# Last output projections by token half: all features of half 0, then all of half 1

## The reference, cut to what matters

```python
for layer in range(DEPTH):
    h = rmsnorm(x, norm_g[layer])
    y = mixer(h, ...)          # each ends in (o * silu(g)) @ w_out
    x = x + y
return rmsnorm(x, final_g)
```

## Time and profile before

| | |
|---|---|
| median of 3 runs | 3079.87 us (3074.44 to 3081.11) |
| the profiled execution | 3079.59 us, span 3077.9 us |
| instructions | 43530 |
| DVE, ACT, POOL busy | 56%, 40%, 20% |
| mean granted clock of PE | 0.927 |
| DMA | 107.89 MB, mean 35 GB/s |
| `w_out` slabs loaded | 8 + 16 + 8 + 8, of 512 KB each |

### The profile page before, as it was taken

One profiled execution on the slowest core, in us unless ns is written; L12 is line 12 of the kernel. 1 busy time (PEld: TensorE's weight loads), 2 busy tenths in 40 slices (PEclk: granted clock), 3 DMA queues, 4 the chain that ended last, 5 costly groups with the idle time before them and its releaser, 6 DMA issues. The chain is left out here.

```text
span 3077.9 us, 43530 instructions
## 1 busy us (share of the span) xinstructions
PE 2506.3 (81%) x17488; PEld 1421.7 (46%) x17488; DVE 1715.5 (56%) x2387; ACT 1242.4 (40%) x1857; POOL 607.9 (20%) x457
## 2 busy tenths in 40 slices
PE   4899878667887977978896888888888779888887
PEld 1566643224544544545553344444344235655543
DVE  5455453465555555555544676676676434455543
ACT  3322332233443433433432566666666423333221
POOL 2000001210000000000022455555555420000001
PEclk8999999788999999999997899999999889999988
DMA  2111000100010000010102110111111001111001
GB/s 83 35 41 36 29 28 28 50 26 13 24 32 30 27 31 19 31 38 15 43 14 62 28 49 28 49 49 42 28 49 35 14 29 35 35 35 35 28 28 69
DMA packets 43036, 107.89 MB, mean 35 GB/s; under 512 B 7986, under 2 KB 13362, under 8 KB 42836
## 3 DMA queue, kind: packets, MB, share of 16 engines
q1 hardware_dynamic: 42836, 105.11, 11.0%
HBM read 84.11 MB, written 4.19 MB: 29 GB/s over the span
## 5 line engine op out<-in xcount | busy, mean ns | idle before, releaser
L219 PE MATMUL psum<-h_hi,gla_w_hi 128*128 128x512 f16 (+1 forms) x544 | 215.9, 397 | 93.0 <-issue 47.8
L1417 ACT ACTIVATE mla_prob<-psum,mla_neg_top 128x128 f32<-128x128 f32 (+7 forms) x128 | 94.9, 741 | 343.3 <-DVE mla_neg_top L1322 343.3
L918 POOL TENSOR_TENSOR sb_al<-sb_zc,sb_ah 128x256 f16<-128x256 f32 (+2 forms) x96 | 171.8, 1790 | 220.5 <-ACT sb_ah L873 220.5
L220 PE MATMUL psum<-h_lo,gla_w_hi 128*128 128x512 f16 (+1 forms) x544 | 215.0, 395 | 0.0
L221 PE MATMUL psum<-h_hi,gla_w_lo 128*128 128x512 f16 (+1 forms) x544 | 214.4, 394 | 0.0
L1339 DVE TENSOR_TENSOR mla_pt_lo<-psum,mla_pt_hi 128x128 f16<-128x128 f32 (+7 forms) x128 | 97.0, 758 | 193.4 <-ACT mla_pt_hi L1425 193.4
L907 POOL TENSOR_TENSOR sb_zc<-sb_zc,sb_el 128x256 f32<-128x256 f32 (+2 forms) x96 | 174.6, 1818 | 137.5 <-ACT sb_el L850 137.4
L1480 POOL TENSOR_TENSOR mla_y_lo<-mla_yt,mla_y_hi 128x512 f16<-128x512 f32 x32 | 37.0, 1157 | 770.8 <-ACT mla_y_hi L1433 770.8
L235 PE MATMUL psum<-gla_w_hi,h_hi 128*128 128x128 f16 x1024 | 173.8, 219 | 11.0 <-issue 11.0
L1211 PE MATMUL psum<-mla_ident,mla_prob 128*128 128x128 f32 x576 | 97.7, 303 | 100.5 <-DVE mla_prob L1334 99.6
L219 PE MATMUL psum<-h_hi,sb_w_hi 128*128 128x512 f16 x384 | 155.0, 404 | 24.9 <-DVE h_lo L384 24.9
(11 more groups left out here) (320 smaller groups left out, 7323.1 us busy)
## 6 DMA issues: line engine op xcount, KB each, us to landing
sb_wf<-in_sb_in SPq DMA_DIRECT2D x32, 512.0 KB, 3.6
gla_wf<-in_gla_v SPq DMA_DIRECT2D x16, 512.0 KB, 3.5
gla_wf<-in_gla_g SPq DMA_DIRECT2D x16, 512.0 KB, 3.5
gla_wf<-in_gla_out SPq DMA_DIRECT2D x16, 512.0 KB, 3.5
mla_wf<-in_mla_gate SPq DMA_DIRECT2D x16, 512.0 KB, 3.4
mla_wf<-in_mla_out SPq DMA_DIRECT2D x16, 512.0 KB, 3.6
xT<-in_x_T SPq DMA_DIRECT2D x8, 512.0 KB, 6.4
gla_wf<-in_gla_q SPq DMA_DIRECT2D x8, 512.0 KB, 3.4
```

The costliest lines, as they stand in the source:

```text
L219: pe.matmul(out, wh[:, w], act_hi[:, k, tok], start=(i == 0), stop=False)
L220: pe.matmul(out, wh[:, w], act_lo[:, k, tok], start=False, stop=False)
L918: pool.tensor_tensor(self.al[s % 2][:, :, off:HALF], self.zc[s % 3][:, :, off:HALF], self.ah[s % 2][:, :, off:HALF], ALU.subtract).then_in ...
L1417: act.activation(self.prob[t % 2][:, 0:w], self.pair(t)[:, 0:w], ACT.Exp, bias=self.neg_top[:, k], scale=self.SCALE, accum_out=self.total[ ...
```

## The change

The last output projection of every layer runs over all feature blocks for token half 0 first, and then over all for half 1. A slab then has one unit (layer 1: two), and every slab is loaded and split twice, once for each half. The first units that are opened early are now half 0 of blocks 0 and 1 (layer 1: 0, 1 and 2), and these belong to two slabs. `finish_items` gets a second bound: ("w", s) stands at the earliest right behind the last item of slab s-2. The buffers of the squares go by k and not by c, and the counts that ACT and POOL wait for follow the new order.

```diff
         for i, it in enumerate(items):
             if it[0] in ("u", "part"):
                 first.setdefault(self.units[it[1]][2], i)
+                last[self.units[it[1]][2]] = i
         for s in where:
-            moved.setdefault(first[s - 1] if s else 0, []).append(("w", s))
+            at = first[s - 1] if s else 0
+            if s >= self.NSPLIT:
+                at = max(at, last[s - self.NSPLIT] + 1)
+            moved.setdefault(at, []).append(("w", s))
...
         act.wait_ge(L.acc_free[b], L.turn[n])
-        i = 2 * k + c
         if k == 0:
             out = L.net.ssum[:, c * HALF:(c + 1) * HALF]
         else:
-            out = self.sq[c][:]
-            if k > 1:
-                act.wait_ge(self.sum_ready, i - 3)
+            out = self.sq[k % 2][:]
+            if k > 2:
+                act.wait_ge(self.sum_ready, self.sums_before(k - 1, c))
+            elif c:
+                act.wait_ge(self.sum_ready, self.sums_before(1, c))
...
+    def sums_before(self, k, c):
+        return c * (KD - 1) + k - 1
...
-        i = 2 * k + c
-        pool.wait_ge(self.sq_ready, i + 1)
-        if i >= 4:
-            pool.wait_ge(self.sum_ready, i - 3)
-        pool.tensor_tensor(s, s, self.sq[c][:], ALU.add).then_inc(self.sum_ready, 1)
+        pool.wait_ge(self.sq_ready, c * KD + k + 1)
+        if k > 1:
+            pool.wait_ge(self.sum_ready, self.sums_before(k, c))
+        pool.tensor_tensor(s, s, self.sq[k % 2][:], ALU.add).then_inc(self.sum_ready, 1)
...
         last = []
-        for k in range(KD):
-            last += L.slab(w_out[k], 1024, [("x", (k, c, True)) for c in range(2)], [5, 6, 7])
+        for c in range(2):
+            for k in range(KD):
+                last += L.slab(w_out[k], 1024, [("x", (k, c, True))], [5, 6, 7])
         early, last = L.open_early(L.cut(last, ("x",)), 2)
...
-    def out_items(self, group, part):
+    def out_items(self, group, part, halves=range(2)):
         final = group == MLA_HEADS // self.GROUP - 1
         items = self.L.slab(self.w["out"][group * 4 + part], 1024,
-                            [("x", (2 * part + k, c, final, group)) for k in range(2) for c in range(2)], self.ACC)
+                            [("x", (2 * part + k, c, final, group)) for k in range(2) for c in halves], self.ACC)
...
         tail = []
-        for part in range(4):
-            tail += self.out_items(MLA_HEADS // self.GROUP - 1, part)
+        for c in range(2):
+            for part in range(4):
+                tail += self.out_items(MLA_HEADS // self.GROUP - 1, part, (c,))
         early, tail = L.open_early(L.cut(tail, ("x",)), 3)
...
     def act_x(self, act, n):
         k, c, final, group = self.L.units[n][1]
-        if final and (k, c) in ((0, 0), (1, 0)):
+        if final and (k, c) in ((1, 0), (2, 0)):
             act.wait_ge(self.rlo, len(self.ropes))
```

More of the change, by code:

```diff
@@ L146, in finish_items @@
         first = {}
+        last = {}
         for i, it in enumerate(items):
@@ L1624, in build_items @@
         last = []
-        for k in range(KD):
-            last += L.slab(self.w["out"][k], 1024, [("x", (k, c, True)) for c in range(2)], self.ACC)
+        for c in range(2):
+            for k in range(KD):
+                last += L.slab(self.w["out"][k], 1024, [("x", (k, c, True))], self.ACC)
         early, last = L.open_early(L.cut(last, ("x",)), 2)
```

## The result

The changed kernel takes 3086.91 us (median of 7 runs, 3083.02 to 3089.5) against 3079.53 us (median of 7, 3074.44 to 3081.11) before. The ratio is 1.0026, its 95% interval 1.0015 to 1.0038: slower by 7.4 us in the medians, with 4.6 to 11.7 us inside the interval. The profiled execution took 3089.5 us, span 3087.8; it is the slowest of the seven, so the two profiles lie 9.9 us apart.

The account below looks back on a forecast made before the run. PE (TensorE) alone was taken to set the four output projections. Stalls of 5.4 us at the first units plus 1.6 for the clock gave +7.0, 3086.6 us; the 8-in-10 range was 3081.0 to 3093.0.

Parts of the forecast that it names:

- The waits: Before the third slab's first unit in each last output projection, PE idles until that slab is split: 5.4 us in sum.
- the wake-up: PE's restart after each of the four pauses: each could be 0.1 us more.
- The order among the waits: First gated 1.31, latent 0.6, stick-breaking 2.28, last gated 1.25 us; stick-breaking longest because the second unit's quarter ran at full clock.
- The steady part at nothing: Later units of the last projections: 28 more loads, high splits and low splits lie beside PE work and cost nothing.
- the cover of 1.19 us: Slack in each later unit: low split ends 3.99 us after the previous unit's end, next boundary comes at 5.18 us.
- the overrun rival: Later boundaries: split lag grows past 5.18 us and PE waits each time; 0.2 us at 48 boundaries, 3095; chance 0.05.
- The clock, one drop of three: After the three pauses over 1 us, one drops PE to half rate: +1.6 us.
- the lower bound of that term: Clock rises while PE idles, so matmuls run at full level later: -0.4 us per pause over 1 us, -1.2 together.
- The first rival: Only the stalls in the last projections, clock untouched: +5.4 us, 3085.0, counting as no change; chance 0.33.
- Early opening of C in the latent layer: The third unit's first quarter, opened early, finds the second slab already split, covered by 1.4 us: no cost.
- The rival on the other side: At layer boundaries the next norm takes half 0 early: 4.9 us at four boundaries, 3065.6; chance 0.04.
- The total: Whole kernel: stalls 5.4 plus clock 1.6 make +7.0 us, 3086.6 us.

Follow-up runs that it names:

- third pair: Changed kernel plus a third pair of split buffers for the last projections' slabs, all extra loads and splits kept: 3078.98 us against 3077.25 for the kernel before.
- loaded twice: Kernel before with its old order of units, but each slab of the last projections loaded and split once per unit: 3087.46 us, ratio 1.0034.

## Why the prediction was right, point by point

- **The waits.** Forecast 1.31, 0.6, 2.28 and 1.25 us, 5.4 in sum. Counted as the forecast counts, from A's add to C's first matmul (E's in the latent layer), the start moved by 1.36, 0.87, 2.39 and 1.30, 5.9 in sum. Three of the four are over by 0.05 to 0.11, the wake-up for which I had allowed 0.1 each. In the latent layer it is 0.27: I took 0.6 although the slower low split gave 0.75, and the slower one it was, 1.45 us. That PE's idle time in the four stretches is 5.4 too is chance: its brackets, 1.59, 0.70, 1.98 and 1.09, start later, and hang on when PE's clock rose during B's quarter. That the wait goes when the buffer does (third pair) and comes with the old order too (loaded twice) shows that it is this dependence.
- **The order among the waits** came out as well, the stick-breaking layer's longest, as B's quarter ran at the higher clock there.
- **The steady part at nothing.** In the gated and stick-breaking layers the cover of 1.19 us held: 1.1 us more in the chain cost nothing, 2.2 cost 0.47 at each boundary. For the latent layer the result is right and the reading wrong. I took 3.99 us of lag from the gated layer and wrote that 1.45 already holds the overlap with GpSimd; there it was 2.3, and 0.08 us of cover were left. That nothing was paid in this layer is luck, and the overrun rival, to which I gave 0.05, was near. Its form, an excess at each boundary, is the right one.
- **The clock, one drop of three.** The drop is in the stick-breaking layer, in all three profiles with this pause of 1.98 or 1.99 us (projection of 78.09 us each), and it costs 1.69 us; the pauses of the gated layers cost none. I had argued for a drop in this layer first, but one in three was a choice in the middle of a range, and that exactly one came is in part luck. In the last gated layer the shift gave back 0.4 (+1.30 at C, +0.88 at the end), the lower bound of that term: two matmuls that ran at 1.2 GHz now come after the rise. So the clock's net share is 1.3 us where I had 1.6, and the waits' 5.9 where I had 5.4: two small misses that partly cancel. The first rival, whose sum the Trainium skill's rule gave ("TensorE: Matmul & The Clock Gate", section "Why this matters for your kernels"), falls here: the page asks for a longer gap than the 1.98 us after which this clock was low, and filling that gap brought the clock back. The measurement decides. It is the trace that decides here: 5.4 us, the rival's sum, lie inside the interval of the times.
- **Early opening of C in the latent layer** waited for nothing: slab 1's low split ended at 1582.70, C's first matmul came at 1584.14, 1.4 us later, as forecast.
- **The rival on the other side,** that half 0 done early would let something start: as the code stood it could not, and the four stretches between a layer's last add and the next norm kept their length (4.85, 5.33, 7.09 and, before the final norm, 3.82 us before; 4.83, 5.32, 7.17 and 3.77 after). Not at the norm but in the branch output lay the gain of that order, and it took an edit of the wait and of the list to reach it: 16 us.
- **The total,** 3086.6 forecast, 3086.91 measured. Such nearness is luck: the runs of one kernel spread over 6 us, and the two terms missed in opposite directions.

## What to carry to other kernels

When each of two buffers comes to serve one unit and no longer two, look at the first units and not at the steady part: units opened early have only their rest to cover the first reuse. A reordering that makes one half ready sooner brings nothing until the waits of that half are narrowed and its work is moved in the list; until then it only pays its price. Doubled transfers and splits may cost nothing where the bound engine never waits for them, and the slack to the next boundary, read from one period of the timeline, says how much more they may grow. Read that slack in every layer that has another chain: here it was 1.19 us in three layers and 0.08 in the fourth.

## What the runs showed of the hardware that I had not expected

- Pauses of PE of nearly one length have different prices: after 1.98 us PE ran at 1.2 GHz for 3.4 us, from about 0.45 us behind the restart on; after 1.59 and 1.09 the granted clock stayed at 1.00; and one and the same pause of 2.7 us in the latent layer was followed by 1.00 in one profile and by 0.64 in another (34.96 against 36.65 us of projection).
- Where a chain on other engines sets PE's restart, the scatter goes. The first gated layer's projection took 76.35 us in the four profiles in which C's start hangs on slab 2's split and the rest runs at the full pace, and so did the last one's; in the kernel before the two took 74.97 and 75.47 in one and the same profile, as PE's clock rose at different moments.
- A low split takes 1.22 us alone, 1.45 where GpSimd's add runs on for its first 0.37 us, and 2.3 where it runs beside GpSimd's adds for 1.2 us: the overlap is lost almost whole. In the chain past the cover the missing overlap made the excess 0.47 and not 0.7 us, and the long overlap used up the latent layer's cover.
